# A retrieval kernel in which every fourth V row leaves TensorE: scaled on ScalarE, summed on GpSimd

## The reference, cut to what matters

```python
def block(tb):                                     # tb: the tokens, (blk, 1024)
    ...                                            # scores, top-16 per half, top-16 of 256 sums
    gate = jax.nn.softmax(top_s, axis=-1)          # 8 heads x 16 experts = 128 picks per token
    pre = jnp.einsum('thkd,td->thk', u_tab[expert], tb)
    act = jax.nn.gelu(pre) * gate
    return jnp.einsum('thk,thkd->td', act, v_tab[expert])
```

## Time and profile before

| | |
|---|---|
| median of 3 runs | 4013.58 us (4000.27 to 4017.56) |
| the profiled execution's own time | 3995.36 us |
| its span, first to last instruction | 3993.6 us |
| busy share: TensorE / VectorE / ScalarE / GpSimd | 81% / 58% / 32% / 30% |
| mean granted clock of TensorE | 0.932 |

### The profile page before, as it was taken

One profiled execution on the slowest core, in us unless ns is written; L12 is line 12 of the kernel. 1 busy time (PEld: TensorE's weight loads), 2 busy tenths in 40 slices (PEclk: granted clock), 3 DMA queues, 4 the chain that ended last, 5 costly groups with the idle time before them and its releaser, 6 DMA issues.

```text
span 3993.6 us, 33306 instructions
## 1 busy us (share of the span) xinstructions
PE 3224.6 (81%) x10460; PEld 1781.8 (45%) x10460; DVE 2297.7 (58%) x5165; ACT 1271.6 (32%) x3644; POOL 1178.3 (30%) x1094
## 2 busy tenths in 40 slices
PE   7667388788889776988998789888899678777776
PEld 6556255445556324744653236544464223222222
DVE  4332687555554787645436758355543886745444
ACT  1211133433232323233333343332333324334333
POOL 0000122234222422222333432223323424434332
PEclk9788699899899988988999999999999989999999
DMA  4103387788889966977999998878999878999997
GB/s 153 42 1 114 122 301 278 266 325 309 324 311 347 355 243 268 334 286 280 352 357 420 391 420 328 306 286 337 372 350 365 341 283 349 390 420 420 418 419 291
DMA packets 183524, 1225.45 MB, mean 307 GB/s; under 512 B 21169, under 2 KB 21441, under 8 KB 48050
## 3 DMA queue, kind: packets, MB, share of 16 engines
q0 software_dynamic: 153088, 1115.26, 72.4%
q1 hardware_dynamic: 30258, 108.05, 7.4%
HBM read 1211.38 MB, written 11.84 MB: 306 GB/s over the span
## 4 chain that ended last, share of the span: by engine, by line
PE 49%; DVE 22%; DMA 16%; ACT 7%; issue 3%; DVEq 2%; POOL 0%; SPq 0%; ACTq 0%; POOLq 0%
PE ps L438 48%; DMA ring<-in_uv,picked 15%; DVE ring L1681 7%; ACT scratch L856 2%; ACT diag L856 2%; DVE scratch L1586 1%; ACT L856 1%; ACT gated L856 1%; DVE scratch L1588 1%; DVE scratch L1584 1%; DVE scratch L1592 1%; DVEq L1582 1%; DVE scratch L1617 1%; DVE scratch L1612 1%; ACT act_v L856 1%
## 5 line engine op out<-in xcount | busy, mean ns | idle before, releaser
L438 PE MATMUL ps<-ring,diag 128*128 128x512 f32 x4160 | 2117.4, 637 | 602.5 <-ACT diag L856 565.3
L423 POOL DMA_INDIRECT ring<-in_uv,picked x1024 | 1114.4, 1088 | 2381.1 <-PE ps L438 2172.0
L1681 DVE SCALAR_TENSOR_TENSOR ring<-ring,htok 128x1024 f32<-128x1024 f32 x1024 | 1241.9, 1226 | 755.1 <-DMA ring<-in_uv,picked 749.5
L438 PEld LDWEIGHTS ps<-ring,diag 128*128 128x128 f32 x4160 | 754.2, 196 | 1654.4 <-ACT diag L856 1017.3
L438 PE MATMUL ps<-hT,wring 128*128 128x256 f32 (+1 forms) x3200 | 743.8, 386 | 36.5 <-DVE hT L1128 21.7
L438 PEld LDWEIGHTS ps<-hT,wring 128*128 128x128 f32 x3200 | 614.2, 192 | 218.7 <-issue 96.8
L856 ACT ACTIVATE act_v<-pre 128x1 f32<-128x1 f32 x1040 | 208.6, 201 | 1543.5 <-DVE ring L1681 1542.4
L856 ACT ACTIVATE diag<-masks,gated 128x128 f32<-128x128 f32 x1024 | 411.0, 401 | 34.8 <-PE ps L438 1.3
L856 ACT ACTIVATE gated<-act_v,gates 128x1 f32<-128x1 f32 x1024 | 301.6, 295 | 33.3
L438 PEld LDWEIGHTS ps<-scratch 128*128 128x128 f32 (+3 forms) x1424 | 192.5, 195 | 112.2 <-issue 63.0
L438 PE MATMUL ps<-scratch 128*128 128x128 f32 (+5 forms) x1424 | 218.6, 298 | 29.2 <-DVE scratch L1273 13.8
(11 more groups left out here) (217 smaller groups left out, 1521.4 us busy)
## 6 DMA issues: line engine op xcount, KB each, us to landing
wring<-in_weights SPq DMA_DIRECT2D x200, 512.0 KB, 6.6
ring<-in_uv,picked POOLq DMA_INDIRECT x1024, 9.0
scratch<-in_keys POOLq DMA_DIRECT2D x4, 1024.0 KB, 11.1
scratch<-in_s_gla POOLq DMA_DIRECT2D x4, 1024.0 KB, 12.4
out_o_gla<-scratch POOLq DMA_DIRECT2D x4, 1024.0 KB, 11.1
xT<-in_xT SPq DMA_DIRECT2D x1, 2080.0 KB
scratch<-in_s_dn POOLq DMA_DIRECT2D x1, 2048.0 KB, 9.5
scratch<-in_s_ssm POOLq DMA_DIRECT2D x1, 2048.0 KB, 16.1
```

Source lines behind the costliest of these rows:

```text
L423: pool.indirect_dma_start(out=ring[:, g % RING, :], out_offset=None, in_=io["uv"][L], in_offset=bass.IndirectOffsetOnAxis(ap=index, axis=0 ...
L438: return pe.matmul(out, lhsT, rhs, start=start, stop=stop)
L1681: stt(x, x, 1.0, h, MUL, MUL, accum_out=pre[:, g % SMALL:g % SMALL + 1]).then_inc(sem("dotted"), 1)
```

## The change

Within the first eight units, tile S excepted, every pick with k % 4 == 2 (`ASIDE`) is treated otherwise: 32 picks in each of six units, 192 of 1040. For such a pick

- ScalarE scales the V half of the slot in place (128x1024) by the weight, instead of making a diagonal (128x128); signal `scaled`;
- TensorE does nothing;
- GpSimd adds the V half to `otok` (a copy for the first pick of a unit), signal `side_done`, and the gather that reuses the slot waits for that. The addition for pick g stands in GpSimd's program behind the gather of pick g + 6.

At the end of these six units VectorE adds banks 0 and 1 to `otok` (`join_out`) in the place of ScalarE's copy. `weighed`, `v_done` and the slot of `diag` count only the remaining picks (`TURNED`).

```diff
+ASIDE = [t != S and u < 8 and k % 4 == 2 for u, (_, t) in enumerate(UNITS) for k in range(COUNT[u])]
+SUMMED = [sum(ASIDE[:g]) for g in range(len(ASIDE) + 1)]
+TURNED = [g - n for g, n in enumerate(SUMMED)]
+HAS_ASIDE = [any(ASIDE[FIRST[u]:FIRST[u + 1]]) for u in range(len(UNITS))]
...
+            def add_v(g):
+                u = [v for v in range(len(UNITS)) if FIRST[v] <= g][-1]
+                v = ring[:, g % RING, D:2 * D]
+                pool.wait_ge(sem("scaled"), SUMMED[g + 1])
+                if SUMMED[g] == SUMMED[FIRST[u]]:
+                    if u:
+                        pool.wait_ge(sem("out_mm"), u)
+                    last = pool.tensor_copy(otok[:, :], v)
+                else:
+                    pool.wait_ge(sem("side_done"), SUMMED[g])
+                    last = pool.tensor_tensor(otok[:, :], otok[:, :], v, ALU.add)
+                last.then_inc(sem("side_done"), 1)
...
-                    if g >= RING:
-                        pool.wait_ge(sem("v_done"), g - RING + 1)
+                    if g >= RING and ASIDE[g - RING]:
+                        pool.wait_ge(sem("side_done"), SUMMED[g - RING + 1])
+                    elif g >= RING:
+                        pool.wait_ge(sem("v_done"), TURNED[g - RING + 1])
...
                     front.upto(g)
+                    if g >= RING - 1 and ASIDE[g - RING + 1]:
+                        add_v(g - RING + 1)
...
-                    pe.wait_ge(sem("weighed"), g + 1)
-                    for h in range(2):
...
+                    if not ASIDE[g]:
+                        pe.wait_ge(sem("weighed"), TURNED[g + 1])
+                        d = TURNED[g] % DIAGS
+                        for h in range(2):
...
-                    f(dst, src, ACT.Copy, scale=gated[:, s:s + 1]).then_inc(sem("weighed"), 1)
+                        f(dst, src, ACT.Copy, scale=gated[:, s:s + 1]).then_inc(sem("weighed"), 1)
+                    else:
+                        act.wait_ge(sem("gated"), g + 1)
+                        v = ring[:, g % RING, D:2 * D]
+                        f(v, v, ACT.Copy, scale=gated[:, s:s + 1]).then_inc(sem("scaled"), 1)
                     front.upto(g)
                     choose.upto(g)
-                act.wait_ge(sem("v_done"), FIRST[u + 1])
+                if HAS_ASIDE[u]:
+                    continue
+                act.wait_ge(sem("v_done"), TURNED[FIRST[u + 1]])
...
+            def join_out(u):
+                dve.wait_ge(sem("v_done"), TURNED[FIRST[u + 1]])
+                dve.wait_ge(sem("side_done"), SUMMED[FIRST[u + 1]])
+                x = otok.rearrange("p (b i) -> p b i", b=2)
+                tt(x, x, ps[:, 0:2, :], ADD).then_inc(sem("otok_ready"), 1)
...
                     stt(x, x, 1.0, h, MUL, MUL, accum_out=pre[:, g % SMALL:g % SMALL + 1]).then_inc(sem("dotted"), 1)
+                    if k == 0 and u and t != S and HAS_ASIDE[u - 1]:
+                        join_out(u - 1)
                     if k == 1 and u:
                         add_out(u - 1)
```

More of the change, by code:

```diff
@@ L832, in _ @@
                     g = FIRST[u] + k
-                    pe.wait_ge(sem("weighed"), g + 1)
-                    for h in range(2):
-                        if t == S:
-                            out, weight = ps[0:NS_TOK, h, :], diag[:, g % DIAGS, 0:NS_TOK]
-                        else:
-                            out, weight = ps[:, h, :], diag[:, g % DIAGS, :]
-                        last = mm(out, weight, ring[:, g % RING, D + 512 * h:D + 512 * h + 512], k == 0, k == COUNT[u] - 1)
-                    last.then_inc(sem("v_done"), 1)
+                    if not ASIDE[g]:
+                        pe.wait_ge(sem("weighed"), TURNED[g + 1])
+                        d = TURNED[g] % DIAGS
+                        for h in range(2):
+                            if t == S:
+                                out, weight = ps[0:NS_TOK, h, :], diag[:, d, 0:NS_TOK]
+                            else:
+                                out, weight = ps[:, h, :], diag[:, d, :]
+                            last = mm(out, weight, ring[:, g % RING, D + 512 * h:D + 512 * h + 512], k == 0, k == COUNT[u] - 1)
+                        last.then_inc(sem("v_done"), 1)
                     if t == S and k + 2 < NS_TOK:
@@ L1071, in _ @@
                     f(gated[:, s:s + 1], act_v[:, s:s + 1], ACT.Copy, scale=gate).then_inc(sem("gated"), 1)
-                    act.wait_ge(sem("gated"), g + 1)
-                    if g >= DIAGS:
-                        act.wait_ge(sem("v_done"), g - DIAGS + 1)
-                    if t == S:
-                        dst, src = diag[:, g % DIAGS, 0:NS_TOK], oneh[:, k * NS_TOK:(k + 1) * NS_TOK]
-                    else:
-                        dst, src = diag[:, g % DIAGS, :], ident
-                    f(dst, src, ACT.Copy, scale=gated[:, s:s + 1]).then_inc(sem("weighed"), 1)
+                    if not ASIDE[g]:
+                        act.wait_ge(sem("gated"), g + 1)
+                        d = TURNED[g]
+                        if d >= DIAGS:
+                            act.wait_ge(sem("v_done"), d - DIAGS + 1)
+                        if t == S:
+                            dst, src = diag[:, d % DIAGS, 0:NS_TOK], oneh[:, k * NS_TOK:(k + 1) * NS_TOK]
+                        else:
+                            dst, src = diag[:, d % DIAGS, :], ident
+                        f(dst, src, ACT.Copy, scale=gated[:, s:s + 1]).then_inc(sem("weighed"), 1)
+                    else:
+                        act.wait_ge(sem("gated"), g + 1)
+                        v = ring[:, g % RING, D:2 * D]
+                        f(v, v, ACT.Copy, scale=gated[:, s:s + 1]).then_inc(sem("scaled"), 1)
                     front.upto(g)
                     choose.upto(g)
-                act.wait_ge(sem("v_done"), FIRST[u + 1])
+                if HAS_ASIDE[u]:
+                    continue
+                act.wait_ge(sem("v_done"), TURNED[FIRST[u + 1]])
                 if u:
@@ L1630, in topk_step @@
                         if t != S:
-                            dve.wait_ge(sem("weighed"), FIRST[v + 1])
+                            dve.wait_ge(sem("gated"), FIRST[v + 1])
                     dst = ids[R, 1, :] if t == S else gates[R, HSLOT[t], :]
```

## The result

The changed kernel takes 4051.41 us (median of 4 runs, 4047.99 to 4070.21), the kernel before 4013.76 on the same chip (4000.27 to 4017.56). The ratio taken over all runs is 1.0115, 95% interval 1.0077 to 1.0153: slower by 1.2%. The prediction, 3940 us and faster, has the wrong sign, and its range, which ended at 4030, doesn't hold the time. The profiled execution has a span of 4052.1 us at a mean granted clock of 0.877, where that of before had 0.932.

The account below looks back on a forecast made before the run. TensorE bounds projections and recurrences, DMA the gather-bound stage, VectorE choice. -70-26-3+11+8+7 = -73 us takes the profiled 3995.4 to 3922, plus 18.2 to the runs' median: 3940 us; range 3860 to 4030.

Parts of the forecast that it names:

- V products gone, projection stages: Five stages where TensorE has no gap: 54 picks set aside save 1.3 us each, 70 us less.
- V products gone, all other stages: Outside projection stages, TensorE's missing V products save 53 us in recurrences and 7 in the first stage.
- additions and unit ends: Dots waiting for GpSimd's additions, plus VectorE's sum replacing the copy at six unit ends (7 us): 57 us more.
- V products gone, recurrence stages: Three stages where TensorE waits briefly: 66 picks set aside save 0.8 us each, bounds 0 and 1.15.
- the clock gives it back: Rival: gaps left by missing products put more picks at TensorE's lower clock, costing 73 us; about 4010 us, chance 0.13.
- no lower than 0.85: Sign: the lowest granted clock of TensorE in recurrences if the forecast holds.
- ScalarE ... so this hides: ScalarE scales 1024 columns in 1.05 us instead of making a diagonal; claimed hidden, as ScalarE is 32% busy.
- The price of the additions: GpSimd's 2.5 us addition holds VectorE's dots, 0.87 us on average; 0.4 counted in recurrences, nothing in projection stages.
- 1 in 6: Sign: the share of dots in recurrences expected to take 2 to 3.7 us.
- the shared read path decides: Rival: additions hold dots on the chain, deciding from 1.1 us per addition; slower, 4160 us at worst, chance 0.15.
- the 0.97 named for it: Sign: DMA share in projection stages of 0.97 or more, with four slots in about 16.0 us.
- The gather behind GpSimd's work: Gathers issued 0.7 us later in recurrences, 1.7 in the gather-bound stage; queueing covers it, 0 us, without cover 50.

Follow-up runs that it names:

- drop: Kernel before with the V rows of the 192 picks set aside left out, neither scaled nor added: 3952.51 us, 0.9857.
- scale_only: `drop` with ScalarE's scaling of the V half kept and the gather waiting for it, nothing added by GpSimd: 3977.31 us, 0.9913.
- drop_fill: `drop` with useless TensorE products by zeros, without a wait, for the 144 picks set aside outside the projection stages: 3923.02 us, 0.9793.
- write_only: Changed kernel with each GpSimd addition replaced by two memsets of the output tile, which read nothing: 3974.97 us, 0.9915.
- after_fill: Changed kernel with useless TensorE products by zeros in place of the 144 V products outside the projection stages: 4065.15 us, 1.0142.
- proj3: Changed kernel with picks set aside only in the five projection stages, every third one, 63 picks, full result: 3947.50 us, 0.9848.

## Why the prediction was wrong

**The sum, term by term, in differences taken from the ratios.** Forecast -73, measured +46; the difference of 119 us has four parts.

| term | forecast | measured | from |
|---|---|---|---|
| V products gone, projection stages | -70 | -64 | the table's row of `drop`, a single execution |
| V products gone, all other stages | -60 | +7 | `drop`, -57, less the -64 |
| ScalarE's scaling | 0 | +22 | `scale_only` less `drop` |
| additions and unit ends | +57 | +81 | changed kernel less `scale_only` |

The forecast's -60 is 66 x 0.8 = 53 in the recurrences and 12 x 0.6 = 7 in the first stage. Its +57 is 66 x 0.4 = 26, 11 + 8 for choice, 12 x 0.4 = 5 and 7 for unit ends. By the medians alone the last three measured terms would be +12, +21 and +69, with the same signs.

**The step that failed** is "V products gone, recurrence stages", 0.8 us a pick by how the products lie on the chain. That working asked what lies beside what, and took each remaining instruction at its old length. The runs showed otherwise: in slots 568 to 656 the stage got longer by 24 us with 89 PE instructions less, at a clock of 0.79 instead of 0.92, and went back to 318 us when useless products brought the clock back. This is the rival "the clock gives it back". It expected some 54 more picks at the lower level, and the trace of `drop` has 69 more. It priced them at 73 us; that forecast and measurement of this term are 67 us apart is not the same quantity, and the likeness is luck. Of the 67 the useless products bring back 26, give or take 20 (some 45 in the profiled executions, outside the projection stages); as they may cost time themselves, the clock's part can be larger. The rival had a chance of 0.13, and the forecast's own test, a clock "no lower than 0.85", fell with 0.77 to 0.81. The argument against it was that TensorE is seldom the bound at low levels; the earlier trace rows already showed it busy for 178 of 210 us in a recurrence, at a clock of 0.98, and TensorE has over half of the chain in slots 568 to 656. Even with the clock held, `drop_fill` gains some 19 us in the recurrences and not 53, and one of its three stages gives nearly all of it, so that 0.8 was also too high: it took a pattern of 9 us, in the first recurrence, for all three.

**"ScalarE ... so this hides"** failed too. The duration was right within a tenth (1.15 against 1.05), but the scaling wasn't free: 22 us, give or take 18. Whether it was ScalarE's queue that didn't cover it, or the gather's longer wait, isn't known.

**The price of the additions** was the right mechanism, too small. A dot waits 0.87 us per addition by the working; measured it is (1.382 - 1.226) x 1024 / 186 = 0.86. That the two agree so closely is in part luck: 111 dots took over 1.5 us, against 6 before, where seven in ten of the additions would be 130, and those that were held waited 1.5 us and not 1.25. In the recurrences 27 of 259 dots took over 2 us, 1 in 10 and not 1 in 6. The addition takes 2.36 us in the median and 2.52 on average, as forecast. What was off is how much of the waiting lands on the chain. Reading costs 80 us, give or take 20, over 192 picks, 0.42 each, of which the projection stages take next to nothing by the table (-53 with memsets, -46 with additions). Outside them it is then about (80 - 7) / 138 = 0.53 a pick, where the prediction had 50 us of waiting in all. The rival "the shared read path decides" wanted 1.1 us; it was right about the sign by another's help, because the gross gain that it had to beat wasn't 123 us but 35 (57 less the 22 of scaling). With a waiting of 0.7 in place of 0.87 the prediction's sum would be some 10 us better and not 7, a fifth of its 50; this changes nothing.

The Trainium skill, "SBUF — State Buffer", section "Who interferes with whom", names this contention as one with GpSimd instructions that read, and not with those that only write. The runs agree with both halves: dots of 1382 ns beside additions, 1307 beside copies, 1225 beside memsets.

**Right steps.** The projection term: 16.2 us for four slots, forecast 16.0, and -64 us for -70; only the DMA share, 0.90 to 0.95, stayed below the 0.97 named for it, and that additions are free there was too kind, since the changed kernel keeps 46 of the 64. The prediction read the clock of saturated stretches as 0.98 to 1.00; the earlier trace rows has 0.97 in one of them. The gather behind GpSimd's work costs nothing that shows, with memsets in the place of the additions: `write_only` and `scale_only` differ by 0.0002. The gather-bound stage grew by 5 to 6 us with additions and by 0 with memsets. The choice stages got longer, as forecast, but by more: 19 us were put down and 10 to 20 named as the sign, and it is 27 by the windows, 24 by the table.

**What stays open:** how the scaling's 22 us divide, and why `after_fill` loses elsewhere what it gains by its clock. Whether a shorter filler in a kernel like `drop_fill` would do as well wasn't tried.

## What to carry to other kernels

Removing TensorE work pays in a stage where TensorE has no gap. In a stage where it waits now and then, look at the granted clock before counting a gain: as in `drop`, fewer instructions may run at the lower level and take nearly as long as the many did. The additions moved to GpSimd weren't paid in GpSimd's time but in that of VectorE's operations with two SBUF operands, so place such work where these are ahead of need. Here one condition on the slots turned a loss of 1.2% into a gain of 1.9% (0.9813, 0.9774 to 0.9853), with more additions per stage than the change had.

## What was unexpected of the hardware

- Useless matmuls made a kernel faster: 576 instructions on a constant tile took `drop` from 3952.51 to 3923.02 us, and the granted clock from 0.875 to 0.924.
- The clock of a stage can differ between two executions without a change in that stage: 0.92 and 317 us before, 0.87 and 331 us in `proj3`.
- A GpSimd copy with a single SBUF operand holds a dot too, though less than an addition with two, and is held by it: 1041 ns at a unit's start, 1191 and 1481 on average beside dots. The longest addition took 5.62 us against a median of 2.36, beside two products of the choice with two SBUF operands and a dot; the second of these products took 4.25 us, the first 2.28.
- Memsets that kept GpSimd busy for 1.9 us a pick cost nothing that could be measured, 3974.97 us against 3977.31 without them.
